# Strassen block products for the three down projections, with the weight sums shared between GpSimd and VectorE

## The reference, cut to what matters

```python
# layer 0: D_FF = 2816
x = x + (jax.nn.silu(gate) * up) @ w_down[l]
# layers 1 and 2: D_FF_2 = 4096
u = jnp.square(jax.nn.relu(jnp.einsum('bsd,df->bsf', h, w_ff1[l])))
x = x + jnp.einsum('bsf,fd->bsd', u, w_ff2[l])
```

## Time and profile before

| what | value |
|---|---|
| median of 3 runs | 1936.46 us (1936.27 to 1937.68) |
| the profiled execution, its span | 1936.4 us |
| TensorE busy | 1906.5 us, 98% of the span |
| VectorE busy | 980.9 us, 51% |
| ScalarE busy | 810.6 us, 42% |
| GpSimd busy | 306.1 us, 16% |
| transfers | 167.78 MB, mean 87 GB/s |
| matmuls of the down projections | 3 x 688, of 9718 in all |

### The profile page before, as it was taken

How to read it: one execution, slowest core, us unless ns; L and a number is a source line. 1 busy time by engine, 2 the same in 40 slices (tenths; PEclk the granted TensorE clock), 3 DMA queues, 4 the chain that set the end, 5 groups by cost and what they waited for, 6 DMA issues and landing times.

```text
span 1936.4 us, 24529 instructions
## 1 busy us (share of the span) xinstructions
PE 1906.5 (98%) x9718; PEld 1594.4 (82%) x9718; DVE 980.9 (51%) x1549; ACT 810.6 (42%) x1424; POOL 306.1 (16%) x378
## 2 busy tenths in 40 slices
PE   9999999999999999999999999999999999999998
PEld 7888778888888888878898888888878788888887
DVE  5566777522233357589842233337668962223334
ACT  4445876422223235277533232223547743323222
POOL 2133344000000010003412220001002312221000
PEclk9999999999999999999999999999999999999999
DMA  7212111233333322221133333332121224333331
GB/s 240 57 56 93 55 44 45 90 103 93 96 97 98 98 79 65 87 88 45 54 120 98 98 96 93 96 96 89 55 88 44 70 73 125 94 98 96 98 98 55
DMA packets 97138, 167.78 MB, mean 87 GB/s; under 512 B 8160, under 2 KB 49152, under 8 KB 97024
## 3 DMA queue, kind: packets, MB, share of 16 engines
q1 hardware_dynamic: 97024, 166.21, 27.6%
HBM read 164.09 MB, written 2.10 MB: 86 GB/s over the span
## 4 chain that ended last, share of the span: by engine, by line
PE 86%; DVE 5%; ACT 4%; POOL 2%; issue 2%; DMA 0%; SPq 0%; DVEq 0%; POOLq 0%; ACTq 0%
PE ps L49 83%; PE ps L52 3%; DVE wlo L71 2%; ACT sk1h L65 1%; POOL p L71 1%; ACT whi L65 1%; ACT p L62 1%; ACT L62 1%; DVE p L91 1%; POOL hTl L71 1%; DMA raw<-in_w_in_dram 0%; DVE pS L91 0%; DVE rot L71 0%; DVE hTl L71 0%; DVE x L71 0%
## 5 line engine op out<-in xcount | busy, mean ns | idle before, releaser
L65 ACT ACTIVATE whi<-raw 128x1024 fp32r<-128x1024 f32 (+1 forms) x294 | 310.0, 1054 | 728.2 <-PE ps L49 725.0
L71 DVE TENSOR_TENSOR wlo<-raw,whi 128x1024 fp32r<-128x1024 f32 (+1 forms) x294 | 361.0, 1228 | 395.1 <-ACT whi L65 392.1
L49 PE MATMUL ps<-hTh,whi 128*128 128x512 f32 (+1 forms) x1176 | 442.3, 376 | 0.0
L49 PE MATMUL ps<-hTh,wlo 128*128 128x512 f32 (+1 forms) x1176 | 437.7, 372 | 0.0
L49 PE MATMUL ps<-hTl,whi 128*128 128x512 f32 (+1 forms) x1176 | 437.6, 372 | 0.0
L49 PE MATMUL ps<-whi,uh 128*128 128x512 f32 x688 | 268.0, 390 | 0.0
L49 PE MATMUL ps<-whi,ul 128*128 128x512 f32 x688 | 267.7, 389 | 0.0
L49 PE MATMUL ps<-wlo,uh 128*128 128x512 f32 x688 | 267.6, 389 | 0.0
L49 PEld LDWEIGHTS ps<-hTh,wlo 128*128 128x128 f32 x1176 | 220.8, 188 | 39.8
L49 PEld LDWEIGHTS ps<-hTh,whi 128*128 128x128 f32 x1176 | 221.0, 188 | 37.1 <-DVE wlo L71 0.4
L49 PEld LDWEIGHTS ps<-hTl,whi 128*128 128x128 f32 x1176 | 221.1, 188 | 36.4
(11 more groups left out here) (243 smaller groups left out, 2290.4 us busy)
## 6 DMA issues: line engine op xcount, KB each, us to landing
raw<-in_w_ff_dram SPq DMA_DIRECT2D x128, 512.0 KB, 3.6
raw<-in_w_gate_up_dram SPq DMA_DIRECT2D x88, 256.0 KB, 3.1
raw<-in_w_in_dram SPq DMA_DIRECT2D x40, 512.0 KB, 4.6
raw<-in_w_in_dram SPq DMA_DIRECT2D x68, 256.0 KB, 3.1
raw<-in_w_down_dram SPq DMA_DIRECT2D x22, 512.0 KB, 3.5
raw<-in_w_o_dram SPq DMA_DIRECT2D x16, 512.0 KB, 4.3
x<-in_x_dram SPq DMA_DIRECT2D x8, 512.0 KB, 6.5
raw<-in_w_out_dram SPq DMA_DIRECT2D x8, 512.0 KB, 3.9
```

The source lines that it names most:

```text
L49: return self.eng.matmul(out, l, r, start=start, stop=stop, skip_group_check=True)
L65: return self.eng.activation(out, in_, ACT.Copy)
L71: return self.eng.tensor_tensor(out, a, b, op)
```

## The change

Rows of the weight matrix are now taken in pairs of 128, tokens in two halves of 256, and columns in two halves of 512. For each pair of rows this is a product of 2 x 2 blocks by 2 x 2 blocks, and it is computed by Strassen's scheme: seven block products M1 to M7 of sums of blocks in place of eight. A block product has two token groups of 128 (`r`), three matmuls each: 42 matmuls for a pair of rows, where it was 48.

The seven results need 14 banks, and there are eight. So there are two sweeps over all pairs. Sweep A makes M4, M1, M6 and M3 (4 x 2 banks), with units made of pairs of rows: `row_pairs` loads both rows of a pair (1 MB) into one of three double buffers (`quads`: the four `raw` buffers and `htmp`, which was the norm's scratch). Of the four blocks of the pair, GpSimd makes two sums in one instruction of 128 x 1024 (`wsA`), then a third of 128 x 512 (`wsB`), and VectorE the fourth of 128 x 512 (`wsC`), all in place. Then come `whi` and `wlo` as before. Sweep B makes M5, M7 and M2, with units of one 512-column block of two pairs of rows (`row_blocks`, loaded again from memory); for M7 GpSimd adds two units (`ysm`).

On the side of the tokens, sweep A needs two plain blocks (`uhr`, role "r") and two differences (`udif`, made by GpSimd in one instruction of 128 x 512, role "s"). Sweep B needs two further differences, which GpSimd makes in place in `u` (`uD` of 128 x 2 x 512 and `uE` of 128 x 2 x 256 for two pairs).

The results are added to `x` with signs: 24 additions for a layer instead of 8, 14 of them between the sweeps. A bank of sweep B may be started when the results of sweep A in it are added. The tables of times for the down projection now come from a planner (`plan_down`) with its own costs. The core of the diff:

```diff
@@ units and their buffers
+    quads = [r.t("raw%d" % i, [128, 4, 512]) for i in range(NR // 2)]
...
+    quads.append(r.t("htmp", [128, 4, 512]))
+    raw = [quads[i // 2][:, :, :].rearrange("p c n -> p (c n)")[:, 1024 * (i % 2):1024 * (i % 2) + 1024] for i in range(6)]
...
+    udif = [r.t("udif%d" % i, [128, 2, 256]) for i in range(2)]
...
+    def row_blocks(w, nk):
+        first = len(plan)
+        for p, n in doubles(nk):
+            v = w[256 * p:256 * (p + n), :].rearrange("(a k p) n -> p a k n", k=2, p=128)
+            for k, c0 in ((1, 512), (1, 0), (0, 0)):
+                plan.append((n, 512, [(0, 512, v[:, :, k, c0:c0 + 512])]))
+        return first
@@ TensorE
+            for p, M, r in pairs_order(m):
+                yield T["dn", m, "A", p, M, r]
+                second = M in ("M6", "M3")
+                unit, b = U["dn", m] + 2 * p + second, DB[m][M][r]
                 pe.wait_ge(*at("wlo", unit))
+                pe.wait_ge(*at("ul", (m, "s" if M in ("M6", "M1") else "r", p)))
...
+                st = us[2 * (p % 2) + (M in ("M6", "M1"))]
+                c0, w0 = 256 * (M in ("M4", "M1")) + 128 * r, 512 * (M in ("M1", "M3"))
+                for a, c in P3:
+                    ins = pe.mm(ps[b][:, :], st[a][:, c0:c0 + 128], (whi, wlo)[c][unit % NS][:, w0:w0 + 512], p == 0 and (a, c) == (0, 0), p == np_ - 1 and a == 1)
+                ins.then_inc(*up("mm", ("dn", m, "A", p, M, r)))
@@ ScalarE
+                if p >= 2:
+                    act.wait_ge(*at("mm", ("dn", m, "A", p - 2, "M3", 1)))
+                act.copyA(us_view(s, 0, 2), u_pair(m, p)).then_inc(*up("uhr", (m, "r", p)))
...
+                act.wait_ge(*at("udf", (m, p)))
+                if p >= 2:
+                    act.wait_ge(*at("mm", ("dn", m, "A", p - 2, "M6", 1)))
+                act.copyA(us_view(2 * (p % 2) + 1, 0, 2), udif[p % 2][:, :, :]).then_inc(*up("uhs", (m, "s", p)))
@@ VectorE
+        def weight_difs(m):
+            for p in range(NK[m] // 2):
+                yield T["wsC", (m, p)]
+                q = quads[RS[U["dn", m] + 2 * p] // 2]
+                dve.wait_ge(*at("wsB", (m, p)))
+                dve.tt(q[:, 0, :], q[:, 3, :], q[:, 1, :], ALU.add).then_inc(*up("wsC", (m, p)))
@@ GpSimd
+                pool.tt(q[:, 1:3, :], q[:, 1:3, :], q[:, 3::-3, :], ALU.add).then_inc(*up("wsA", (m, p)))
...
+                pool.wait_ge(*at("wsA", (m, p)))
+                pool.tt(q[:, 3, :], q[:, 0, :], q[:, 3, :], ALU.subtract).then_inc(*up("wsB", (m, p)))
...
+                if p >= 2:
+                    pool.wait_ge(*at("ul", (m, "s", p - 2)))
+                pool.tt(udif[p % 2][:, :, :], bc(u[:, 2 * p, 0:256], 1, [128, 2, 256]), u[:, 2 * p:2 * p + 2, 256:512], ALU.subtract).then_inc(*up("udf", (m, p)))
```

More of the change, by code:

```diff
@@ new lines, in x_key, with pairs_order, units_b, blocks_order @@
+    def x_key(m, M, r):
+        return [k for M_, r_, _, _, _, k in x_sums(m) if (M_, r_) == (M, r)][-1]
+    def pairs_order(m):
+        np_ = NK[m] // 2
+        order = [(p, M, r) for p in range(np_ - 2) for M in MA for r in range(2)]
+        return order + [(p, M, r) for M in MA for r in range(2) for p in (np_ - 2, np_ - 1)]
+    def units_b(m):
+        n = 0
+        for p, k in doubles(NK[m]):
+            for M in MB:
+                yield n, M, p, k
+                n += 1
+    def blocks_order(m):
+        units = list(units_b(m))
+        order = [(n, r) for n in range(len(units) - 3) for r in range(2)]
+        a, b, c = range(len(units) - 3, len(units))
+        return order + [(a, 0), (b, 0), (a, 1), (b, 1), (c, 0), (c, 1)]
@@ new lines, in raw_after, with k_of, y_of @@
+    def raw_after(m, i):
+        after = [("wlo", RP[i])] if RP[i] is not None else []
+        after += [("wsC", k_of(RP[i]))] if k_of(RP[i]) else []
+        after += [("ysm", y_of(RP[i]))] if y_of(RP[i]) else []
+        return after + [("up", m, 1, 0, 0)] * (RS[i] >= 4)
+    def k_of(i):
+        for m in range(3):
+            if i is not None and U["dn", m] <= i < U["dB", m] and (i - U["dn", m]) % 2 == 0:
+                return m, (i - U["dn", m]) // 2
+    def y_of(i):
+        for m in range(3):
+            if i is not None and U["dB", m] <= i < U["end", m] and (i - U["dB", m]) % 3 == 0:
+                return m, i - U["dB", m] + 1
@@ L960, in totals, with summed, u_pair, u_block @@
         return hf[:, h, 256 - (1024 >> lv):256 - (512 >> lv)]
+    def summed(i):
+        for m in range(3):
+            if U["dn", m] <= i < U["dB", m]:
+                p, second = divmod(i - U["dn", m], 2)
+                return ("wsC" if second else "wsB"), (m, p)
+            if U["dB", m] <= i < U["end", m] and (i - U["dB", m]) % 3 == 1:
+                return "ysm", (m, i - U["dB", m])
+        return None
+    def u_pair(m, p):
+        v = u[:, 2 * p:2 * p + 2, :].rearrange("p k (c n) -> p (k c) n", c=2)
+        return v[:, 0:4:3, :]
+    def u_block(m, n):
+        _, M, p, k = list(units_b(m))[n]
+        v = u[:, 2 * p:2 * (p + k), :].rearrange("p (a k) n -> p a k n", k=2)
+        return v[:, :, 1 if M == "M7" else 0, 256:512] if M == "M2" else v[:, :, 1 if M == "M7" else 0, 0:256]
+    def us_view(s, part, n):
+        return us[s][part][:, 0:256 * n].rearrange("p (c n) -> p c n", c=n)
     def sp_program(sp):
```

333 lines of the change are left out of this document (251 added, 82 removed).

## The result

The changed kernel takes 2228.7 us (median of four runs, 2225.9 to 2229.3) against 1937.1 us of the kernel before on the same chip: ratio 1.150, 95% interval 1.149 to 1.152. The forecast was 2055 us, range 1985 to 2090. The direction was right; the size was 174 us short.

The account below looks back on a forecast made before the run. TensorE, busy for 98% of the span, was taken as the bound. Layer 0 +24.4, layers 1 and 2 +84.0, boundaries +8 and the end of layer 2 +2.5 made +118.9 on 1936.4: 2055 us, range 1985 to 2090.

Parts of the forecast that it names:

- What is saved, 58.5 us: Down projections: 43 pairs of rows at 42 matmuls instead of 48, 410.0 us for 468.5, if TensorE stays fed.
- Turns: GpSimd and VectorE exclude each other for whole instructions reading two SBUF operands; VectorE's turns 1.07 us for 1024, 0.55 for 512.
- rival 2: The exclusion does not bind in-place, strided instructions; TensorE stays the bound and the kernel gets faster, 1894 us; chance 0.05.
- 1024 is not shown, and on the line through 256 and 512 it is 0.90 + 2 x 0.41 = 1.72: GpSimd's turn for 1024 numbers, extrapolated from 0.49 us for 256 and 0.90 for 512; bounds 1.31 and 2.0.
- between the floor of 17.3 and this chain I take 19.0: Sweep A, two pairs: 17.3 us of turns, or 19.4 with a 6.9 us TensorE wait and clock loss; 19.0 taken.
- TensorE bounds it: Sweep B, two pairs: 6.6 us of VectorE and GpSimd work against 8.2 us of matmuls.
- The 14 additions between the sweeps hide under the last blocks of A: VectorE's additions between sweeps A and B were set at no cost.
- the 2 us for banks: Layer 0: 2 us for banks that wait for VectorE's 14 additions of 0.69 us.
- The clock: Sweep A: each long TensorE wait is followed by 3.2 us at 0.50 clock, losing 1.6 us every two pairs.
- Rival 3: TensorE sinks to the 1.2 GHz level for most of sweep A: +180 us on the forecast, 2235 us; chance 0.05.
- Boundaries: Between layers 3 us without work, taken as 4, twice; the end of layer 2 another 2.5; bounds 2 and 20 together.
- Rival 1: Turns alone: the exclusion holds but no time is lost between turns and the clock stays up, 2015 us; chance 0.24.

Follow-up runs that it names:

- tiny_replanned: Changed kernel with GpSimd's sums cut to one column (product not computed), replanned at 0.2 us a sum and higher matmul costs: 1907.0 us, ratio 0.984.
- same_operand: Changed kernel with each GpSimd sum reading one input twice instead of two different views (product not computed): 2176.6 us, ratio 1.124.
- replanned_gpsimd: Changed kernel, same instructions; planner books GpSimd's sums on VectorE's resource, with higher matmul costs and transfers at 3.5 us: 2084.8 us, ratio 1.076.
- pe_cost_085: Changed kernel, same instructions; the planner counts three matmuls as 0.85 us instead of 0.681, which changes the order: 2150.8 us, ratio 1.110.
- dma_adds: Changed kernel with two of a pair's four combined blocks made by accumulating DMAs, all other sums on VectorE, replanned: 2027.1 us, ratio 1.046.

## Why the forecast was wrong in size

Six runs form a table of medians in us:

| sums made by | planned with the change's cost for TensorE | planned with costs nearer the measured | difference |
|---|---|---|---|
| GpSimd (and `wsC` by VectorE) | 2228.7 | 2084.8 | 143.9 |
| VectorE | 2109.2 | 1978.9 | 130.3 |
| hardly anyone | 2071.0 | 1907.0 | 163.9 |

So the 291 us over the kernel before are -31 (fewer matmuls, after the boundaries), +178 (GpSimd's sums in the better order) and +144 (order, with the clock that its waits cost). The last is a lower bound, since no order was shown to be the best: with VectorE's sums two further plans took off another 30 us.

Step by step:

- **What is saved, 58.5 us.** The count of matmuls was right. `tiny_replanned` shows what is left of it: the three stages are 45 us shorter (116.8, 155.4 and 154.3 against 121.7, 176.1 and 174.2), the profiled executions as a whole 33 us, so 12 us are given back at their ends. Of the 13 us missing inside the stages 11 are in layer 0's sweep B.
- **Turns.** The rule was right, and held for in-place, strided and broadcast operands too, so rival 2 falls. VectorE's turns were right to 0.01 us.
- **The step "1024 is not shown, and on the line through 256 and 512 it is 0.90 + 2 x 0.41 = 1.72" failed**, and with it 0.90 for 512. 2.20 and 1.12 were measured; the upper bound of 2.0 was too low as well. The trace of before had an instruction of 512 numbers with two different inputs that took 1.28 us (`mixR<-mixR,sg`), and I had read the ones with 1.04. `same_operand` puts 52 us on this. The Trainium skill ("GPSIMD Engine Reference", section "Elementwise — side-by-side cycle accounting") has 2.6 cycles an element, from which 2.2 us for 1024 is an estimate. The trace agrees (2.34 to 2.36 alone, 2.20 as a turn). I had set this aside for rows of another kind of operand.
- **The step "between the floor of 17.3 and this chain I take 19.0" failed.** I followed one wait of the list, 6.9 us every double pair. In the middle of sweep A the trace has 7.4 and 10.8 us in turn: behind the block of `ul` and `udif` whole sums of 2.20 us got their turn ahead of the `wlo` that TensorE waited for. With the measured turns the floor was 19.8 and the loop 22.1.
- **The step "TensorE bounds it" for sweep B failed.** VectorE's and GpSimd's work there was below TensorE's 8.2 us, as I had counted, but in layers 1 and 2 ScalarE's list put `uh` ahead of `whi`. In the changed kernel an `uh` waits until 1476.00, two `whi` stand behind it, and TensorE waits 4.72 us, until 1480.62. One cost in the planner, 0.85 for 0.681, took 22 us off sweep B in layer 1 with no instruction changed. A sum of work by engine can't see this; the list has to be followed in sweep B as I had in A.
- **The step "The 14 additions between the sweeps hide under the last blocks of A" failed in layer 0**, and with it the 2 us for banks there. VectorE's list has splits of later units ahead of the additions; TensorE waited 6.39 us, until 733.11, and worked at 0.50 for 3.5 us after it. So its sweep B took 59.0 us for 44.9 us of matmuls: 6.4 for this wait, some 1.8 for the clock after it, 4.8 for waits on `wlo`, the rest in smaller pieces.
- **The clock.** 1.6 us a double pair was forecast; over 21.5 double pairs it is 54 us, 2.5 each, and less in the middle of the sweep. With waits filled at least 35 of the 54 us come back, and the kernel gains 28. Rival 3's 2235 us lies near the measured time by chance: the clock in sweep A was 0.78 and 0.79, not 0.50.
- **Boundaries.** 10.5 us were taken and about 19 measured (289.8 for the profiled executions, less 739.4 - 468.5 for the stages), within their bounds. Where 3 us without work were expected between layers it was 7.5 (the next layer's first matmul comes 7.5 us after the last down matmul, where it came 0.23 after before).

Rival 1, turns alone, was a good description of `replanned_gpsimd`: its 2015 us plus 2.5 us for the true turns in each of some 21.5 double pairs is 2069, against 2084.8.

What stays open: how the 144 us of order divide between the lists of GpSimd, ScalarE and VectorE; `pe_cost_085` moved all of them. And whether a tail that finishes token groups one after another, as before, would give back the 12 us at the ends; it wasn't tried.

## What to carry to other kernels

Where two engines exclude each other, a helper is worth having only if its turn is shorter than the other's own time for the job: here 1.12 against 0.55 us, so moving sums to GpSimd cost twice what VectorE would have paid. Price an instruction from rows with the same kind of operands, not only the same size; where an estimate and the nearest row differ, look for a row with the operands of the case in hand. A planner that writes a fixed order must be fed measured times of all engines, TensorE's waits among them: with costs that are too low, waiting work is put ahead of ready work, and here that cost at least 144 us where the fewer matmuls gave 31.

## What the runs showed of the hardware that I had not expected

- GpSimd takes 1.04 us for 512 and 1.90 for 1024 numbers if both inputs are the same data, and 1.26 and 2.36 us if they are two different tiles or views. A second input that repeats one number along a row also gave 1.04 us for 512 (`p<-p,small`).
- In the changed kernel TensorE's waits of 2.67 us (at 604.5) and 10.81 us (at 1295.8) were followed by 3.2 and 3.4 us of work at the 1.2 GHz level (0.50 granted), as the wait of 2.2 us by 3.2. After other waits of sweep A the work at 0.50 took longer, but not in the order of their length: 5.4 us after 8.73 (at 1256.93), 6.2 after 8.47 (at 1372.12), 4.5 after 12.82 (at 1394.27).
- In a window of 100 us of `dma_adds`' sweep A, accumulating transfers of 256 KB, issued by GpSimd, landed after 4.6 and 4.9 us (medians for `raw` and `htmp`), no sooner than the loads of twice the size beside them (4.8 and 4.6 us). The DMA engines were busy for 74% of the time, and GpSimd and VectorE waited for transfers.
